# Delta-rule heads: token-major outputs, squares summed by ScalarE, modulation tiles turned for VectorE, and the filling shifted

## The chip, the cores and the metric

One core of a Trainium2 chip runs the kernel. The metric is the device time of one execution in microseconds, as a median of several. The core's engines run side by side, each through its own queue in order: TensorE (PE) for products and transposes, VectorE (DVE), ScalarE (ACT), GpSimd (POOL), and SyncE (SP), which issues most of the transfers. They meet by semaphores.

## The reference

Two transformer blocks over 512 tokens of width 1024. The change lies in the first block's mixer, a gated delta rule with 8 heads of width 128:

```python
qkv = jax.nn.silu(causal_depthwise_conv(p[..., Q_OFF:Z_OFF], gdn_conv_w))
q = l2_normalize(qkv[..., Q_OFF:K_OFF].reshape(b, s, GDN_HEADS, GDN_DK))
k = l2_normalize(...)
v = ...
g = -jnp.exp(a_log) * jax.nn.softplus(p[..., A_OFF:BETA_OFF] + dt_bias)
beta = jax.nn.sigmoid(p[..., BETA_OFF:SCB_OFF])
o = gated_delta_rule_chunked(q, k, v, g, beta)
o = rms_norm(o, gdn_norm_w) * jax.nn.silu(z)
```

In each chunk a triangular system is inverted (t_inv), and then a state of 128 x 128 is carried from chunk to chunk; o is the output. Six rows of modulation per block come from mod = c_act @ w_ada + b_ada, and a final pair from w_ada_f.

## The kernel before, in words

The heads run one after the other: a loop over heads 0 to 6 (stage HEAD), then head 7 written out (stage LAST). Within a head the 512 tokens are four chunks of 128 columns; part(v, n) is chunk n of a [128, 512] tile, bank(b) is one of eight PSUM banks of 512 floats. q, k and v lie with their channels on the partitions (gd q_s, k_s, v_s).

TensorE goes through PE_STEPS in order: kv_tokens (k and v transposed to token rows), g_rows, kk_qk, kb_rows, x_pairs (gd_u_t transposed), then for six levels n the steps y_n, x_n, u_n that invert the triangular matrices by doubling, w, then for each chunk v_new and o, then o_sums (the sum over channels of the squared output, four products with one moving column, and in the same bank six more with one column that sum ada_s, the modulation products that GpSimd has multiplied and added up), and o_norm_rows (the norm factors S_ON spread over rows by four transposes). Every step counts up the semaphore g_pe; the other engines have lists of their own (DVE_STEPS, ACT_STEPS, POOL_STEPS) with g_dve, g_act and g_pool.

Between these steps TensorE does filling: products that the next head (or the gates) needs, with a list of how many quarters stand ahead of which step (HEAD_FILL, LAST_FILL). A weight tile is [128, 8, 128] in two parts w_hi and w_lo and gives 24 products of 512 columns, in four quarters of six. The loop's head has eight tiles, 32 quarters. Tile t writes bank t % 2. The first quarter of a tile waits for the tile's w_lo and for the bank: out_used[b] counts how often the bank's content was consumed.

```python
if q == 0:
    pe.wait_ge(lo_ready, tile.before + 1)
    open_out(stage.out(j, i))
```

Tiles 1, 2 and 3 of a loop head are q, k and v of the next head. Their consumers are a scaled copy by ScalarE (conv_tap) and three taps by VectorE (conv_taps), each of which adds a shifted multiple of the bank to the copy; the third counts up out_used. On VectorE the q taps stand behind the copy of y1 (n == 1), the k taps behind the copy of x2, the v taps behind the copy of y4. Tiles 4 and 5 are the short convolution's, tile 6 a gate (tanh by ScalarE), tile 7 is z. Counted from 0, the quarters 5 to 7 stand at x_pairs, 8 at y0, 9 at x0, 10 at y1, 11 at x1, 12 at y2, 13 at x2 and so on; 12 opens tile 3.

The steps of the output: ScalarE squares o (channel-major, bank 3) into gd dec, VectorE adds the square of q, TensorE sums over channels, VectorE adds a constant (o_mean), GpSimd raises to -1/2 (o_norm), TensorE spreads it over rows into bank 6, and VectorE multiplies o by z and then by bank 6 (o_gate, o_scale), splits the product into og_hi and og_lo. In between it splits w_lo of a coming tile (ahead).

Of the kernel before, what the change touches and what calls it, by code (L numbers as in the profile page):

```python
# [187 lines left out]
LAST_FILL = dict(HEAD_FILL, y1=2, y2=2, y3=2, y4=2, y5=2, v_new0=2, o_sums=3)  # L190
# [44 lines left out]
def block_kernel(nc, a, out):  # L235
# [41 lines left out]


# [5 lines left out]
    with ctx:  # L284
# [396 lines left out]


# [39 lines left out]
        def _(act):  # L722
# [165 lines left out]
            def head(stage, i, h):  # L888
# [1643 lines left out]
```

## Time and profile before

| | us |
|---|---|
| median of 3 runs | 2262.08 |
| lowest, highest | 2258.78, 2263.14 |
| span of the profiled execution | 2261.5 |
| TensorE busy | 2186.9 (97%) |
| VectorE busy | 1319.8 (58%) |
| ScalarE busy | 851.1 (38%) |
| GpSimd busy | 550.0 (24%) |

The heads lie from about 96 us to 708 us of the span. The page's shares are means over stages; a timeline gives each instruction's start and duration and, in brackets, how long its engine had been idle ahead of it and what released it. Matmuls overlap, so their pace is read from start to start: two filling products are 0.23 us apart though each is shown as 0.39 us long. PEclk in a window is the granted TensorE clock as a share of 2.4 GHz.

### The profile page before, as it was taken

To read this page: it belongs to the slowest core of one execution; us is meant where nothing else is said; L and a number is where in the kernel's file an instruction comes from. 1 tells how busy PE (TensorE), PEld (TensorE's weight loads), DVE (VectorE), ACT (ScalarE), POOL (GpSimd) and SP (SyncE) were. 2 spreads that over 40 slices of the span, in tenths; PEclk is the share of its full clock that TensorE was granted. 3 is DMA by queue.
4 is the path that set the end of the run, shared out by engine and by line. 5 is a ranking of instruction groups with operands and counts; after the bars stand their busy time and mean duration, and the time that the engine had idled before them with its cause. 6 is when DMAs were issued, how large, how long until landed. Compare 5 with 4: busy or idle time off the path is not lost.

```text
span 2261.5 us, 30878 instructions
## 1 busy us (share of the span) xinstructions
PE 2186.9 (97%) x10744; PEld 1803.5 (80%) x10744; DVE 1319.8 (58%) x1846; ACT 851.1 (38%) x1248; POOL 550.0 (24%) x571
## 2 busy tenths in 40 slices
PE   5799999999999999999999999999899999999998
PEld 3688888888888878888888888888777777888886
DVE  6667666766654444434457665544588867656432
ACT  3232323233223223223224554532466645445322
POOL 0378777777770040000010000001000000000011
PEclk8899999999999999999999999999999999999999
DMA  6333333333333332333332333333211123333332
GB/s 245 119 102 101 93 97 111 89 96 98 112 94 93 112 112 84 93 102 93 93 94 86 101 95 95 98 96 93 65 57 57 54 68 93 94 102 93 95 96 70
DMA packets 352577, 216.97 MB, mean 96 GB/s; under 512 B 8648, under 2 KB 342914, under 8 KB 350979
## 3 DMA queue, kind: packets, MB, share of 16 engines
q1 hardware_dynamic: 344019, 188.47, 28.3%
q0 software_dynamic: 7968, 27.27, 4.1%
q8 instruction: 39, 0.64, 0.1%
q10 hardware_dynamic: 528, 0.40, 0.1%
q14 instruction: 23, 0.19, 0.0%
HBM read 211.92 MB, written 4.19 MB: 96 GB/s over the span
## 4 chain that ended last, share of the span: by engine, by line
PE 80%; DVE 12%; issue 3%; ACT 2%; DMA 1%; SPq 0%; DVEq 0%; POOL 0%; POOLq 0%; ACTq 0%
PE ps L2027 23%; PE ps L2029 23%; PE ps L2028 23%; PE ps L2198 5%; DVE w_lo L1202 2%; PE ps L2054 1%; DVE small L1911 1%; DMA ada<-w_ada 1%; DVE a_sb L1944 1%; DVE a_t_lo L1920 1%; ACT at_swap L1105 1%; DVE gd_q_g L1498 1%; DVE prob L1939 1%; DVE gd_q_s L1398 1%; DVE gd_y_t L1510 1%
## 5 line engine op out<-in xcount | busy, mean ns | idle before, releaser
L2027 PE MATMUL ps<-h_hi,w_hi 128*128 128x512 f32 x1896 | 773.5, 408 | 15.9 <-DVE gd_q_s L1398 6.3
L2029 PE MATMUL ps<-h_hi,w_lo 128*128 128x512 f32 x1896 | 746.9, 394 | 0.0
L2028 PE MATMUL ps<-h_lo,w_hi 128*128 128x512 f32 x1896 | 745.3, 393 | 0.0
L1202 DVE TENSOR_TENSOR w_lo<-raw,w_hi 128x1024 fp32r<-128x1024 f32 x336 | 452.6, 1348 | 364.3 <-ACT w_hi L730 363.7
L730 ACT ACTIVATE w_hi<-raw 128x1024 fp32r<-128x1024 f32 x336 | 355.5, 1059 | 637.4 <-PE ps L2029 602.3
L2027 PEld LDWEIGHTS ps<-h_hi,w_hi 128*128 128x128 f32 x1896 | 361.2, 190 | 90.2 <-issue 21.9
L2029 PEld LDWEIGHTS ps<-h_hi,w_lo 128*128 128x128 f32 x1896 | 359.7, 190 | 78.0
L2028 PEld LDWEIGHTS ps<-h_lo,w_hi 128*128 128x128 f32 x1896 | 361.3, 191 | 65.6
L2027 PE MATMUL ps<-act_hi,w_hi 128*128 128x512 f32 x528 | 206.0, 390 | 0.0
L2029 PE MATMUL ps<-act_hi,w_lo 128*128 128x512 f32 x528 | 205.5, 389 | 0.0
L2028 PE MATMUL ps<-act_lo,w_hi 128*128 128x512 f32 x528 | 205.4, 389 | 0.0
L598 POOL TENSOR_TENSOR sq_sum<-x 128x512 f32<-128x512 f32 x4 | 4.2, 1039 | 758.6 <-DVE x L1738 488.6
L639 POOL TENSOR_TENSOR ada_w<-ada_w 128x256 f32<-128x256 f32 x144 | 131.9, 916 | 11.3
L2029 PEld LDWEIGHTS ps<-act_hi,w_lo 128*128 128x128 f32 x528 | 99.1, 188 | 20.8
L2027 PEld LDWEIGHTS ps<-act_hi,w_hi 128*128 128x128 f32 x528 | 99.1, 188 | 20.5
L2028 PEld LDWEIGHTS ps<-act_lo,w_hi 128*128 128x128 f32 x528 | 99.1, 188 | 20.1
L639 POOL TENSOR_TENSOR ada_w<-ada_w,cact 128x512 f32<-128x512 f32 x96 | 110.3, 1149 | 3.1 <-DMA ada_w<-w_ada 2.0
L930 ACT ACTIVATE gd_u_t<-ps 128x512 f32<-128x512 f32 x48 | 28.7, 598 | 181.8 <-PE ps L2198 181.8
L1694 DVE TENSOR_TENSOR tmp<-ps,sq_tmp 128x512 f32<-128x512 f32 x44 | 30.4, 691 | 89.3 <-PE ps L2029 82.7
L602 POOL TENSOR_TENSOR sq_tmp<-x 128x512 f32<-128x512 f32 x24 | 25.9, 1079 | 232.6 <-DVE x L1738 149.2
L632 POOL DMA_DIRECT2D ada_w<-w_ada x64 | 51.0, 797 | 83.2 <-DVE g_tok L1381 41.7
L712 POOL TENSOR_TENSOR small<-small 128x4 f32<-128x4 f32 x8 | 8.1, 1007 | 252.4 <-DVE small L1970 252.4
(352 smaller groups left out, 2839.7 us busy)
## 6 DMA issues: line engine op xcount, KB each, us to landing
raw<-ffn_w_up SPq DMA_DIRECT2D x88, 512.0 KB, 3.8
raw<-w_in SPq DMA_DIRECT2D x72, 512.0 KB, 3.8
raw<-w_ffn_in SPq DMA_DIRECT2D x44, 512.0 KB, 3.8
ada_w<-w_ada POOLq DMA_DIRECT2D x64, 256.0 KB, 3.4
raw<-ffn_w_down SPq DMA_DIRECT2D x32, 512.0 KB, 3.7
raw<-diff_w_qkv SPq DMA_DIRECT2D x24, 512.0 KB, 3.7
ada<-w_ada SPq DMA_DIRECT2D x8, 1024.0 KB, 13.3
ada_w<-w_ada_f POOLq DMA_DIRECT2D x32, 256.0 KB, 3.3
```

What stands on the lines that cost most here:

```text
L602: nc.gpsimd.tensor_tensor(sq_tmp[:], x[:, m], x[:, m], MULT).then_inc(sq_own, 1)
L632: nc.gpsimd.dma_start(ada_w[:, half], src).then_inc(ada_land[half], 16)
L639: nc.gpsimd.tensor_tensor(dst, a, b, op).then_inc(ada_own, 1)
L730: nc.scalar.activation(w_hi[:, tile.slot], raw[:, tile.raw], ACT.Copy).then_inc(hi_ready, 1)
L930: nc.scalar.activation(gd["u_t"][:], bank(6), ACT.Copy).then_inc(g_act, 1)
L1105: swapped = nc.scalar.activation(at["swap"][32 * q:32 * q + 32], ps[32 * (q ^ 1):32 * (q ^ 1) + 32, b, :], ACT.Copy)
L1202: nc.vector.tensor_tensor(w_lo[:, tile.slot], raw[:, tile.raw], w_hi[:, tile.slot].bitcast(F32), SUB)\
L1694: nc.vector.tensor_tensor(gs, bank(b), sq_tmp[:], MULT).then_inc(out_used[b], 1)
L2027: nc.tensor.matmul(dst, w_hi[:, tile.slot, k], hi, start=first, stop=False)
L2028: nc.tensor.matmul(dst, w_hi[:, tile.slot, k], lo, start=False, stop=False)
L2029: return nc.tensor.matmul(dst, w_lo[:, tile.slot, k], hi, start=False, stop=last)
L2198: ins = nc.tensor.matmul(part(bank(b), n), part(lhs, n), part(rhs, n), start=True, stop=True)
```

## The change

Each output chunk is now token-major (tokens on the partitions), in a bank of its own (O_BANK). Its squares are summed by ScalarE along the row (accum_out), and so are those of q, for which q is transposed to token rows as well (q_tokens, bank 7, behind x_pairs). So o_norm needs no product; the factor S_ON is one number per partition and chunk, VectorE applies it (o_scale), TensorE transposes the result back (o_turn), and VectorE multiplies by z (o_gate). ada_s is transposed by TensorE (ada_turns) and summed along the row by VectorE. GpSimd waits for ada_turns ahead of the next head. Of the filling, one quarter goes from the end of the head to x_pairs: x_pairs has 4, and ada_turns, in the place of o_sums, has 1.

```diff
-PE_STEPS = ["kv_tokens", "g_rows", "kk_qk", "kb_rows", "x_pairs"]
+PE_STEPS = ["kv_tokens", "g_rows", "kk_qk", "kb_rows", "x_pairs", "q_tokens"]
...
-ACT_STEPS = ["k_squares", "exp_decay", "exp_g", "exp_g_rows", "exp_last", "exp_left", "q_squares", "x_pairs"]
+ACT_STEPS = ["k_squares", "exp_decay", "exp_g", "exp_g_rows", "exp_last", "exp_left", "x_pairs", "q_squares"]
...
-    DVE_STEPS += [f"y{_n}"] + (["kbeg_scale", "v_beta", "k_beg"] if _n == 0 else []) + _x
+    DVE_STEPS += [f"y{_n}"] + (["kbeg_scale", "v_beta", "k_beg"] if _n == 0 else ["q_sum"] if _n == 1 else []) + _x
...
-PE_STEPS += ["o_sums", "o_norm_rows"]
-DVE_STEPS += ["o_sum", "o_mean", "ada", "ada_f", "o_gate", "g_col", "o_scale", "o_lo"]
-
-
-
-HEAD_FILL = {name: 1 for name in PE_STEPS if name not in [f"u{_n}" for _n in range(LEVELS - 1)]}
-HEAD_FILL.update(kb_rows=2, x_pairs=3, o_sums=2)
-LAST_FILL = dict(HEAD_FILL, y1=2, y2=2, y3=2, y4=2, y5=2, v_new0=2, o_sums=3)
+PE_STEPS += ["ada_turns", "o_turn"]
+DVE_STEPS += ["o_mean", "ada_sum", "ada_f_sum", "ada", "ada_f", "o_scale", "g_col", "o_gate", "o_lo"]
+
+
+
+HEAD_FILL = {name: 1 for name in PE_STEPS if name not in ["q_tokens"] + [f"u{_n}" for _n in range(LEVELS - 1)]}
+HEAD_FILL.update(kb_rows=2, x_pairs=4)
+LAST_FILL = dict(HEAD_FILL, y1=2, y2=2, y3=2, y4=2, y5=2, v_new0=2, ada_turns=2)
 LAST_FILL["w"] = LAST_FILL["u5"] = 1
-LAST_FILL["o_norm_rows"] = 40 - (sum(LAST_FILL.values()) - LAST_FILL["o_norm_rows"])
+LAST_FILL["o_turn"] = 40 - (sum(LAST_FILL.values()) - LAST_FILL["o_turn"])
...
+    O_BANK = (3, 5, 6, 7)
...
+                pool.wait_ge(g_pe, step(PE_STEPS, "ada_turns", h))
...
-                nc.scalar.activation(gd["q_sq"][:], gd["q_s"][:], ACT.Square, scale=P * 1e-3).then_inc(g_act, 1)
...
+                after_pe("q_tokens")
+                for n in range(NC):
+                    q_sq = nc.scalar.activation(part(gd["q_sq"], n), part(bank(7), n), ACT.Square, scale=(P * EPS) ** 0.5,
+                                                accum_out=small[:, S_QSQ + n:S_QSQ + n + 1])
+                q_sq.then_inc(g_act, 1)
...
-                after_pe(f"o{NC - 1}")
-                nc.scalar.activation(gd["dec"][:], bank(3), ACT.Square).then_inc(g_act, 1)
+                for n in range(NC):
+                    after_pe(f"o{n}")
+                    o_sq = nc.scalar.activation(part(gd["dec"], n), part(bank(O_BANK[n]), 0), ACT.Square,
+                                                accum_out=small[:, S_OSQ + n:S_OSQ + n + 1])
+                o_sq.then_inc(g_act, 1)
...
-                after_dve("o_scale")
+                after_dve("o_gate")
...
+                    if n == 1:
+                        after_act("q_squares")
+                        nc.vector.tensor_scalar(col4(S_QSQ), col4(S_QSQ), P * EPS * 4 * EPS, None, ADD).then_inc(g_dve, 1)
...
-                nc.vector.tensor_tensor(gd["dec"][:], gd["dec"][:], gd["q_sq"][:], ADD).then_inc(g_dve, 1)
-                after_pe("o_sums")
-                nc.vector.tensor_scalar(col4(S_OMS), bank(5)[:, 0:NC], P * EPS * 4 * EPS, None, ADD).then_inc(g_dve, 1)
-                nc.vector.tensor_tensor(mod[:, bass.ds(4 * h + 16, 4)], bank(5)[:, 8:12],
+                nc.vector.scalar_tensor_tensor(col4(S_OMS), col4(S_OSQ), 1.0 / P, col4(S_QSQ), MULT, ADD).then_inc(g_dve, 1)
+                after_pe("ada_turns")
+                nc.vector.tensor_reduce(small[:, S_ADA:S_ADA + 4], chunks(bank(2)), AX_X, ADD).then_inc(g_dve, 1)
+                nc.vector.tensor_reduce(small[:, S_ADA + 4:S_ADA + 6], chunks(bank(4))[:, 0:2], AX_X, ADD).then_inc(g_dve, 1)
+                own("ada_sum")
+                nc.vector.tensor_tensor(mod[:, bass.ds(4 * h + 16, 4)], small[:, S_ADA:S_ADA + 4],
                                         vec[:, bass.ds(4 * h + (V_BADA + 16), 4)], ADD).then_inc(g_dve, 1)
-                nc.vector.tensor_tensor(mod[:, bass.ds(2 * h + 48, 2)], bank(5)[:, 12:14],
+                own("ada_f_sum")
+                nc.vector.tensor_tensor(mod[:, bass.ds(2 * h + 48, 2)], small[:, S_ADA + 4:S_ADA + 6],
                                         vec[:, bass.ds(2 * h + V_BADAF, 2)], ADD).then_inc(g_dve, 1)
-                dve.wait_ge(cv_dve, 10 * h + 10)
-                nc.vector.tensor_tensor(gd["low"][:], bank(3), gd["z_g"][:], MULT).then_inc(g_dve, 1)
+                dve.wait_ge(g_pool, step(POOL_STEPS, "o_norm", h))
+                nc.vector.tensor_scalar(part(gd["low"], 0), part(bank(O_BANK[0]), 0), small[:, S_ON:S_ON + 1], None, MULT)
+                nc.vector.tensor_tensor(chunks(gd["low"][:])[:, 1:NC], ps[:, O_BANK[1]:O_BANK[1] + NC - 1, 0:P],
+                                        spread(col4(S_ON))[:, 1:NC], MULT).then_inc(g_dve, 1)
                 nc.vector.tensor_copy(col4(S_G), head_cols(g_tok, h + 1 if more else h)).then_inc(g_dve, 1)
                 if more:
                     ahead(6)
-                after_pe("o_norm_rows")
-                own("o_gate")
-                nc.vector.tensor_tensor(gd["low_d"][:], gd["low"][:], bank(6), MULT).then_inc(g_dve, 1)
+                dve.wait_ge(cv_dve, 10 * h + 10)
+                after_pe("o_turn")
+                nc.vector.tensor_tensor(gd["low_d"][:], bank(6), gd["z_g"][:], MULT).then_inc(g_dve, 1)
...
-                pe.wait_ge(g_dve, last_head("o_gate", h))
+                pe.wait_ge(g_dve, last_head("o_scale", h))
...
-                pe.wait_ge(g_dve, last_head("o_scale", h))
+                pe.wait_ge(g_dve, last_head("o_gate", h))
...
+                by_chunk(7, q_s, None, True).then_inc(g_pe, 1)
...
-                        nc.tensor.matmul(part(bank(3), n), state[:], part(gd["q_g"], n), start=True, stop=False)
-                    o = nc.tensor.matmul(part(bank(3), n), part(y_t, n), part(gd["qk_t"], n), start=n == 0, stop=True)
+                        nc.tensor.matmul(part(bank(O_BANK[n]), 0), part(gd["q_g"], n), state[:], start=True, stop=False)
+                    o = nc.tensor.matmul(part(bank(O_BANK[n]), 0), part(gd["qk_t"], n), part(y_t, n), start=n == 0, stop=True)
...
-                fill("o_sums")
-                after_dve("o_sum")
-                for n in range(NC):
-                    nc.tensor.matmul(bank(5)[:, n:n + 1], part(gd["dec"], n), cst[:, C_MEAN:C_MEAN + 1], start=True, stop=True)
+                fill("ada_turns")
                 pe.wait_ge(g_pool, step(POOL_STEPS, "ada", h))
                 for j in range(6):
-                    s = nc.tensor.matmul(bank(5)[:, 8 + j:9 + j], ada_s[:, j], one_col, start=True, stop=True)
-                s.then_inc(g_pe, 1)
-                fill("o_norm_rows")
-                pe.wait_ge(g_pool, step(POOL_STEPS, "o_norm", h))
-                rows_of(6, S_ON).then_inc(g_pe, 1)
+                    t = turn(part(bank(2 if j < 4 else 4), j % 4), ada_s[:, j])
+                t.then_inc(g_pe, 1)
+                fill("o_turn")
+                after_dve("o_scale")
+                by_chunk(6, gd["low"], None, True).then_inc(g_pe, 1)
```

TensorE, loop head, the places around step x1. gd_x_t,gd_dia is the end of the products y1, gd_y_t,gd_u_t and gd_u_t,gd_y_t are x1 and u1. Before, from the last filling product at x1 on:

```order
L2028 MATMUL ps<-h_lo,w_hi 128x512
L2029 MATMUL ps<-h_hi,w_lo 128x512
L2188 REGISTER_ALU
L2191 REGISTER_ALU [waits g_dve]
L2198 MATMUL ps<-gd_y_t,gd_u_t 128x128 [waits g_act]
L2198 MATMUL ps<-gd_y_t,gd_u_t 128x128 x3
L2198 MATMUL ps<-gd_u_t,gd_y_t 128x128 x4
L2036 REGISTER_ALU
L2027 MATMUL ps<-h_hi,w_hi 128x512 [waits out_used1,lo_ready]
L2028 MATMUL ps<-h_lo,w_hi 128x512
L2029 MATMUL ps<-h_hi,w_lo 128x512
```

Now, from the products y1 on:

```order
L2207 REGISTER_ALU [waits g_pool]
L2217 MATMUL ps<-gd_x_t,gd_dia 128x128 [waits g_dve]
L2217 MATMUL ps<-gd_x_t,gd_dia 128x128 x3
L2055 REGISTER_ALU
L2046 MATMUL ps<-h_hi,w_hi 128x512 [waits out_used1,lo_ready]
L2047 MATMUL ps<-h_lo,w_hi 128x512
L2048 MATMUL ps<-h_hi,w_lo 128x512
L2046 MATMUL ps<-h_hi,w_hi 128x512
L2047 MATMUL ps<-h_lo,w_hi 128x512
L2048 MATMUL ps<-h_hi,w_lo 128x512
L2207 REGISTER_ALU
```

The filling product that waits for out_used1, the first of tile 3, stood behind x1 and u1 and now stands ahead of them, right behind y1.

VectorE, the same place: gd_y_t<-ps,cst copies the result of y1, and the L1398 rows are the three q taps. Before:

```order
L1510 TENSOR_TENSOR gd_y_t<-ps,cst 128x512 [waits g_pe]
L1393 ISA
L1398 ISA [waits cv_act]
L1398 SCALAR_TENSOR_TENSOR gd_q_s<-ps,vec,gd_q_s 128x511
L1397 ISA
L1398 ISA [waits cv_dve]
L1398 SCALAR_TENSOR_TENSOR gd_q_s<-ps,vec,gd_q_s 128x510
L1397 REGISTER_ALU
L1398 ISA [waits cv_dve]
L1398 SCALAR_TENSOR_TENSOR gd_q_s<-ps,vec,gd_q_s 128x509
```

Now (the taps are L1408):

```order
L1520 TENSOR_TENSOR gd_y_t<-ps,cst 128x512 [waits g_pe]
L1471 REGISTER_ALU
L1523 TENSOR_SCALAR small<-small 128x4 [waits g_act]
L1403 ISA
L1408 ISA [waits cv_act]
L1408 SCALAR_TENSOR_TENSOR gd_q_s<-ps,vec,gd_q_s 128x511
L1407 ISA
L1408 ISA [waits cv_dve]
L1408 SCALAR_TENSOR_TENSOR gd_q_s<-ps,vec,gd_q_s 128x510
L1407 REGISTER_ALU
L1408 ISA [waits cv_dve]
L1408 SCALAR_TENSOR_TENSOR gd_q_s<-ps,vec,gd_q_s 128x509
```

The taps stay where they were, with one small addition (q_sum) ahead of them.

TensorE, end of a loop head. Before, the end of the filling at o_sums and the two sums:

```order
L2028 MATMUL ps<-h_lo,w_hi 128x512
L2029 MATMUL ps<-h_hi,w_lo 128x512
L2188 REGISTER_ALU
L2266 MATMUL ps<-cst,gd_dec 128x1 [waits g_dve]
L2266 MATMUL ps<-cst,gd_dec 128x1 x3
L2267 REGISTER_ALU
L2269 MATMUL ps<-cst,ada_s 128x1 [waits g_pool]
L2269 MATMUL ps<-cst,ada_s 128x1 x5
```

Now, behind the one quarter at ada_turns, its transposes, the quarter at o_turn and the transposes of gd_low:

```order
L2284 REGISTER_ALU
L2073 MATMUL ps<-cst,ada_s 128x128 [waits g_pool]
L2073 MATMUL ps<-cst,ada_s 128x128 x5
L2046 MATMUL ps<-h_hi,w_hi 128x512
L2047 MATMUL ps<-h_lo,w_hi 128x512
L2048 MATMUL ps<-h_hi,w_lo 128x512
L2046 MATMUL ps<-h_hi,w_hi 128x512
L2047 MATMUL ps<-h_lo,w_hi 128x512
L2048 MATMUL ps<-h_hi,w_lo 128x512
L2207 REGISTER_ALU
L2073 MATMUL ps<-cst,gd_low 128x128 [waits g_dve]
L2073 MATMUL ps<-cst,gd_low 128x128 x3
```

The ten products of one column are gone, and the last transposes wait for g_dve (o_scale) in place of g_pool (o_norm).

## Rows read from the trace of the kernel before

**Rows 1.** The page, busy time by engine and the chain that ended last, by engine.

```profile
PE 2186.9 (97%) x10744; PEld 1803.5 (80%) x10744; DVE 1319.8 (58%) x1846; ACT 851.1 (38%) x1248; POOL 550.0 (24%) x571
...
PE 80%; DVE 12%; issue 3%; ACT 2%; DMA 1%; SPq 0%; DVEq 0%; POOL 0%; POOLq 0%; ACTq 0%
```

**Rows 2.** Windows: stretch, us, busy us and instructions by engine, clock, DMA.

```profile
319.60:394.40 74.80, 73.78 (x432) 63.10 (x431) 51.00 (x79) 22.12 (x43) 57.00 (x63) 0.98 0.35 100
394.40:467.90 73.50, 72.55 (x433) 61.93 (x432) 50.24 (x76) 22.09 (x42) 56.26 (x62) 1.00 0.33 93
616.30:708.00 91.70, 91.02 (x505) 77.90 (x504) 45.39 (x74) 28.09 (x39) 49.00 (x55) 0.98 0.30 86
386.50:390.00 3.50, 3.50 (x12) 2.75 (x11) 2.36 (x5) 1.19 (x2) 3.34 (x4) 0.52 0.24 54
```

**Rows 3.** Timeline of TensorE, end of a head: start, us, instructions [idle, releaser].

```profile
457.93 0.95 PE L2266 MATMUL ps<-cst,gd_dec 128*128 128x1 f32 x8
...
460.08 0.49 PE L2027 MATMUL ps<-h_hi,w_hi 128*128 128x512 f32 x1
```

**Rows 4.** Timeline of TensorE around the gd_u_t transposes and the step y1.

```profile
403.09 0.39 PE L2029 MATMUL ps<-h_hi,w_lo 128*128 128x512 f32 x1
403.81 0.65 PE L2054 MATMUL ps<-cst,gd_u_t 128*128 128x128 f32 x4 [0.34 <-DVE gd_u_t L1495]
404.22 0.48 PE L2027 MATMUL ps<-h_hi,w_hi 128*128 128x512 f32 x1
...
411.47 1.05 PE L2198 MATMUL ps<-gd_x_t,gd_dia 128*128 128x128 f32 x8
412.28 0.48 PE L2027 MATMUL ps<-h_hi,w_hi 128*128 128x512 f32 x1
...
415.85 0.47 PE L2027 MATMUL ps<-h_hi,w_hi 128*128 128x512 f32 x1 [0.15 <-DVE gd_q_s L1398]
```

**Rows 5.** Groups by line and shape, TensorE, seven loop heads: busy, mean ns | idle before.

```profile
L2198 PE MATMUL ps<-gd_y_t,gd_u_t 128*128 128x128 f32 x280 | 38.3, 280 | 2.3 <-DVE gd_y_t L1510 1.8
```

**Rows 6.** Timeline of VectorE around the step y1.

```profile
412.56 0.69 DVE L1510 TENSOR_TENSOR gd_y_t<-ps,cst 128x512 f32<-128x512 f32 x1 [1.45 <-PE ps L2198]
413.17 0.74 DVE L1398 SCALAR_TENSOR_TENSOR gd_q_s<-ps,vec,gd_q_s 128x511 f32<-128x511 f32 x1
414.06 1.64 DVE L1398 SCALAR_TENSOR_TENSOR gd_q_s<-ps,vec,gd_q_s 128x510 f32<-128x510 f32 x2 [0.15 <-DVE gd_q_s L1398]
...
416.21 3.02 DVE L1202 TENSOR_TENSOR w_lo<-raw,w_hi 128x1024 fp32r<-128x1024 f32 x1
```

**Rows 7.** The tap line L1398, who waited for it: us, times.

```profile
  PE ps L2027: 6.3, 8
```

**Rows 8.** Timeline of TensorE behind three waits outside the heads.

```profile
74.29 0.77 PE L2027 MATMUL ps<-h_hi,w_hi 128*128 128x512 f32 x1 [5.19 <-DVE gd_q_s L1398]
...
79.12 0.56 PE L2029 MATMUL ps<-h_hi,w_lo 128*128 128x512 f32 x1
...
90.44 0.50 PE L2027 MATMUL ps<-h_hi,w_hi 128*128 128x512 f32 x1 [2.58 <-ACT gd_th L869]
...
846.34 0.76 PE L2027 MATMUL ps<-h_hi,w_hi 128*128 128x512 f32 x1 [2.53 <-DVE h_lo L1266]
...
850.74 0.47 PE L2028 MATMUL ps<-h_lo,w_hi 128*128 128x512 f32 x1
```

**Rows 9.** Timeline of ScalarE and of GpSimd at the end of a head.

```profile
455.37 0.60 ACT L966 ACTIVATE gd_dec<-ps 128x512 f32<-128x512 f32 x1 [9.37 <-PE ps L2258]
...
457.47 0.79 POOL L632 DMA_DIRECT2D ada_w<-w_ada  x1 [1.45 <-issue]
460.51 1.03 POOL L680 TENSOR_TENSOR small<-small 128x4 f32<-128x4 f32 x1 [2.25 <-DVE small L1581]
```

**Rows 10.** Timeline of ScalarE in the last head, behind the step u4.

```profile
659.43 0.60 ACT L930 ACTIVATE gd_u_t<-ps 128x512 f32<-128x512 f32 x1 [6.19 <-PE ps L2198]
...
660.87 0.59 ACT L886 ACTIVATE x<-ps 128x512 f32<-128x512 f32 x1
```

More of the change, by code:

```diff
@@ L75 @@
 S_POOL, S_SHSQ, S_SQX = 68, 72, 73
+S_OSQ, S_QSQ, S_ADA = 80, 84, 88
 S_MAX, S_NEG, S_SUM, S_REC, S_L = 16, 20, 24, 28, 32
@@ L182 @@
     DVE_STEPS += [f"v_new{_n}"] + ([f"state{_n}"] if _n < NC - 1 else [])
-PE_STEPS += ["o_sums", "o_norm_rows"]
-DVE_STEPS += ["o_sum", "o_mean", "ada", "ada_f", "o_gate", "g_col", "o_scale", "o_lo"]
-HEAD_FILL = {name: 1 for name in PE_STEPS if name not in [f"u{_n}" for _n in range(LEVELS - 1)]}
-HEAD_FILL.update(kb_rows=2, x_pairs=3, o_sums=2)
-LAST_FILL = dict(HEAD_FILL, y1=2, y2=2, y3=2, y4=2, y5=2, v_new0=2, o_sums=3)
+PE_STEPS += ["ada_turns", "o_turn"]
[3 more added lines that the diff above has]
+LAST_FILL = dict(HEAD_FILL, y1=2, y2=2, y3=2, y4=2, y5=2, v_new0=2, ada_turns=2)
 LAST_FILL["w"] = LAST_FILL["u5"] = 1
-LAST_FILL["o_norm_rows"] = 40 - (sum(LAST_FILL.values()) - LAST_FILL["o_norm_rows"])
+LAST_FILL["o_turn"] = 40 - (sum(LAST_FILL.values()) - LAST_FILL["o_turn"])
 LAST_FILL["tail"] = 8
-assert sum(HEAD_FILL.values()) == 32 and sum(LAST_FILL.values()) == 48 and LAST_FILL["o_norm_rows"] in (1, 2)
+assert sum(HEAD_FILL.values()) == 32 and sum(LAST_FILL.values()) == 48 and LAST_FILL["o_turn"] in (1, 2)
 ATT_PE = ["scores0", "scores1", "v_turn", "scores2", "scores3"] + [f"turn{_q}" for _q in range(NC)] + ["pv", "sums", "rows"]
@@ L309, in block_kernel @@
         cact = sb("cact", [P, 2, KD])
-        small = sb("small", [P, 80])
+        small = sb("small", [P, 96])
         alog = sb("alog", [P, H])
@@ L932, in head @@
                     if more and n == 0:
-                        after_pe("kk_qk")
                         after_dve("q_g")
@@ L978, in head @@
                     ahead(7)
-                    after_dve("o_gate")
                     act.wait_ge(sc_dve, 3 * h + 3)
```

## The prediction

> **What bounds the kernel now.** I read the page's busy shares and its chain first [rows 1]: TensorE is busy 97% of the span, and the chain that ended last runs through it for 80%. So a change counts by what it does to TensorE's own sequence: work put on it or taken off, and stretches in which it waits. The other engines matter through the waits alone. Next the windows of single head iterations [rows 2]: one takes 73.50 us at a granted clock of 1.00, or 74.80 us at 0.98. The difference of 1.3 us has a place. Right behind the products with one moving column (the o sums and the ada sums) the clock reads 0.52 for a stretch, which is the 1.2 GHz level beside the usual 2.4. Four of the seven loop iterations read 74.8 or 74.9 us and 0.98 in this way (one of them stands in the rows), and the last head, too, reads 0.98: five such stretches in all. Last I read TensorE's timeline through one iteration for the waits that are left in it [rows 4, 5].
>
> **Own work of TensorE, per head.** Removed: the o sums and the ada sums, from 457.93 to the next filling product at 460.08 [rows 3], 2.15 us. Added: six transposes of ada_s and four of q_s. Four transposes take 0.41 us start to start (403.81 to 404.22) [rows 4], so ten take 1.03. The four transposes of S_ON and the four of gd_low cost the same and cancel; the o products swap their operands and keep count and shape. Sum: -1.1 us a head, -8.8 us for eight, all of it on the path. (The Trainium skill, TensorE: Matmul & The Clock Gate, section Terms, calls the transpose mode four times faster for FP32. The row shows 0.10 us for a transpose, and eight FP32 passes of 128 columns, four products, take 0.81 (411.47 to 412.28) [rows 4], so here it is twice. With the page's factor the ten would cost 0.5 us and the kernel would end 4 us earlier. I go by the row.)
>
> **The filling that moves.** This is the term that decides. A head's filling is 32 quarters of six products, four quarters to a weight tile; tiles go to banks 0 and 1 in turn. The first quarter of a tile waits until the bank's last tile has been consumed. With x_pairs at 4 in place of 3, each later quarter stands one slot earlier, and so does each of those waits. I went through them tile by tile. Tile 3 (bank 1) opened at y2, behind the products x1 and u1. Now it opens at x1, right behind y1. Bank 1 is released by the third q tap of VectorE, which stands on VectorE behind the copy of y1 to gd_y_t. The rows give the price: the y1 products start at 411.47 and TensorE is free again at 412.28, 0.81 later [rows 4]. VectorE copies y1 from 412.56 and runs the three taps from 413.17 to about 415.7 [rows 6]; TensorE's next filling starts at 415.85 [rows 4] and names the tap as what it waited for, as it does in all seven heads and once before them [rows 7]. So the bank comes free 4.38 us after y1's start, which the shift of the filling doesn't change, since VectorE waits for y1 itself. New wait: 4.38 - 0.81 = 3.57, and the small q_sum that now stands between copy and taps adds some 0.07: **+3.6 us a head**, seven times. Before, x1, u1 and a quarter of filling lay over it and 0.15 was left idle (0.3 start to start).
>
> Tile 4 (bank 0) opens at x3 in place of y4, and waits for the k taps in the same way, but from x2 there lie u2, a quarter and y3 on TensorE (0.89 + 0.81 + 1.4 + 0.9 = 4.0 us) against 1.1 + 0.6 + 2.65 = 4.35 us on VectorE: +0.3. Tiles 5 to 7 are consumed several microseconds before their new slots. In the last head tile 3 waits for the first step of the short convolution (about 0.3) and tile 6 for the tanh on ScalarE behind u4, which ends 660.87 + 0.59 while u4's copy starts at 659.43 [rows 10], against one quarter and y5's first on TensorE: about +0.9 once.
>
> Waits that go: the transposes of gd_u_t start 0.72 us after the filling product ahead of them, not 0.23 (403.09 to 403.81) [rows 4]: 0.49, which the fourth quarter covers. The waits for gd_y_t at x0 and x2 are 2.3 us in seven heads as idle [rows 5]; idle reads 0.15 less than start to start at each, so 0.55 a head. With the 0.3 at tile 3: -1.3 us a head.
>
> **The end of a head.** Before, no wait stood ahead of the rows of S_ON in most heads. Now TensorE does a quarter, six transposes, a quarter, and then needs gd_low. Counted from the end of the last o product: the last square, a quarter of the 0.60 us square of before with an accumulator read behind it [rows 9], 0.4 as an estimate, o_mean 0.2, the power on GpSimd 1.03 [rows 9], so S_ON is there at about 1.8. But o_scale stands on VectorE behind the ada sums, which wait for the transposes: 1.46 + 0.65 + 0.25 to see them = 2.35; two reductions of 512 and 256 elements from PSUM at the pace of the y copy (0.61 for 512 [rows 6]) 0.95; two small adds, each behind a wait, 0.35; o_scale in two pieces 0.7; 0.1 to TensorE: 4.45. TensorE is there at 1.46 + 0.65 + 1.46 = 3.6. New wait **+0.85 a head** (0.3 to 1.4). In the last head o_turn has two quarters and covers it. The squares, now in pieces with accumulator reads, lie on ScalarE, idle there for 9.37 us before; the added 0.5 us is hidden.
>
> **The clock.** The products of one column go, and with them the five half-speed stretches at 1.3 us: -6.5. The new wait of 3.6 us takes their place. Rows on idling: after 5.19 us of waiting for the same tap ahead of the heads, the products run slowly from 74.29 to 79.12, eleven gaps of 0.44 us where 0.23 is usual; after 2.53 us of idling they do so from 846.34 to 850.74 [rows 8]. That is half speed for 4.4 to 4.8 us, 2.2 us lost; behind the thin products 1.3 us was lost. I take 1.7 for each of seven heads: +11.9. (The Trainium skill, TensorE: Matmul & The Clock Gate, section HAM oscillation — how this bites in real kernels, says that idle gaps drop the clock again and that each costs a slow restart; the two gaps of rows 8 agree. By that rule all seven waits pay.)
>
> **Sum.** A loop head: -1.1 - 1.3 + 3.6 + 0.3 + 0.85 = +2.35; seven: +16.4. Clock: 11.9 - 5.2 = +6.7. Last head: -1.1 - 0.8 (old waits) - 1.3 + 0.3 + 0.9 = -2.0. Total +21. The profiled execution is its span of 2261.5 us, 0.6 under the median of 2262.08, so 2261.5 + 21 = 2282.5; I say **2282**.
>
> **Rivals.**
> - No half speed after the waits: one wait of 2.58 us, ahead of 90.44, was followed by products at the usual pace [rows 8], so the clock does not answer every gap. Then 2261.5 + 16.4 - 5.2 - 2.0 = 2271. At 2.2 us for each it is 2286.
> - The new wait isn't there, because bank 1 comes free before y1. Then the kernel gets faster: -8.8 own work, -1.0 a head of old waits (-8), -6.5 of clock, +0.85 x 7 = +6: 2261.5 - 17 = 2244. GpSimd takes a little of it back: its last ada transfer is issued at 457.47 and lasts 0.79 [rows 9], till 458.26, while the transposes would be due near 458.1. For it: TensorE's idle at that place is 0.15 us only. Against it: VectorE's order puts the taps behind the copy of y1, and that copy waits for y1. It decides if the wait stays under 0.4 us a head.
> - The wait is there but half as long, as VectorE catches up, and the clock holds: 16.4 - 7 x 1.8 - 5.2 - 2.0 = -3.4, 2258 to 2262, no change to be seen.
> - VectorE gets later, not earlier: its copies into SBUF share time with GpSimd's sums (w_lo took 3.02 us at 416.21 [rows 6]); if o_scale and the taps are each 0.5 us later, +7: 2290.
>
> **Chances.** Forecast with the clock at 1.3 to 2.2 us a wait 0.72; full speed after the waits 0.10; later VectorE 0.06; half wait 0.05; no wait 0.07. A measurement of this kernel tells about 0.2% (4.5 us) from no change. Faster 0.07, same 0.05, slower 0.88. The range runs from full speed after the waits, with 3 us for the terms' error, to the late VectorE: 2268 to 2292.
>
> **What would show it.** In each loop head of the changed profile an idle of about 3.4 us ahead of the filling behind y1, released by the q tap; a granted clock near 0.5 behind it, and none behind the ada transposes; no wait at the gd_u_t transposes; about 0.7 us idle ahead of the gd_low transposes, released by VectorE; loop heads of about 76.5 to 77.5 us against 73.5 to 74.8. I am wrong if the bank's release comes from somewhere ahead of y1, if the clock falls for longer than the stretches seen, or if o_scale is more than 1.4 us late.

## The result, and the profile after

The changed kernel takes 2272.67 us (median of four, 2271.41 to 2279.05) against 2262.36: a ratio of 1.0048, 95% interval 1.0035 to 1.0061. It is slower, as forecast and inside the range, but by 10.3 us where the forecast had 20. Its profiled execution has a span of 2269.3 us, 7.8 more than the one before.

The page after, with the parts that answer to [rows 1]:

```profile
PE 2170.7 (96%) x10664; PEld 1793.9 (79%) x10664; DVE 1319.2 (58%) x1870; ACT 861.4 (38%) x1360; POOL 538.1 (24%) x571
...
PE 86%; DVE 7%; issue 2%; ACT 2%; DMA 1%; SPq 1%; DVEq 0%; POOL 0%; POOLq 0%; ACTq 0%
```

TensorE is at 96% where it was at 97%, with less busy time (2170.7 us against 2186.9) in a longer span. So its work has shrunk and its waits have grown. The list of who waited for the tap line, now L1408, says for which (before: [rows 7]):

```profile
  PE ps L2046: 29.5, 8
```

29.5 us instead of 6.3. Of that 5.19 is the wait ahead of the heads, as before; the other seven are one for each loop head, about 3.5 us. TensorE's timeline through one head, in the columns of [rows 3, 4] (start, duration, instructions, idle and releaser):

```profile
410.13 0.60 PE L2073 MATMUL ps<-cst,gd_u_t 128*128 128x128 f32 x4
410.57 0.60 PE L2073 MATMUL ps<-cst,gd_q_s 128*128 128x128 f32 x4
...
417.83 1.05 PE L2217 MATMUL ps<-gd_x_t,gd_dia 128*128 128x128 f32 x8
422.36 0.47 PE L2046 MATMUL ps<-h_hi,w_hi 128*128 128x512 f32 x1 [3.47 <-DVE gd_q_s L1408]
...
465.49 0.82 PE L2073 MATMUL ps<-cst,ada_s 128*128 128x128 f32 x6
466.06 0.47 PE L2046 MATMUL ps<-h_hi,w_hi 128*128 128x512 f32 x1
...
468.69 0.66 PE L2073 MATMUL ps<-cst,gd_low 128*128 128x128 f32 x4 [1.00 <-DVE gd_low L1606]
```

Read from start to start: y1's products start at 417.83 and TensorE could go on 0.81 later, as before [rows 4]; the next filling starts at 422.36, that is 4.53 us after y1's start and 3.72 us later than it could. The gd_u_t transposes come without a wait. Six ada transposes take 0.57 us (465.49 to 466.06). The gd_low transposes start 1.00 us (idle) late. VectorE in the same two places:

```profile
418.92 0.69 DVE L1520 TENSOR_TENSOR gd_y_t<-ps,cst 128x512 f32<-128x512 f32 x1 [1.43 <-PE ps L2217]
419.53 0.24 DVE L1523 TENSOR_SCALAR small<-small 128x4 f32<-128x4 f32 x1
419.68 0.74 DVE L1408 SCALAR_TENSOR_TENSOR gd_q_s<-ps,vec,gd_q_s 128x511 f32<-128x511 f32 x1
420.57 1.64 DVE L1408 SCALAR_TENSOR_TENSOR gd_q_s<-ps,vec,gd_q_s 128x510 f32<-128x510 f32 x2 [0.15 <-DVE gd_q_s L1408]
...
466.34 0.69 DVE L1595 TENSOR_REDUCE small<-ps 128x4 f32<-128x512 f32 x1 [1.48 <-PE ps L2073]
466.95 0.41 DVE L1596 TENSOR_REDUCE small<-ps 128x2 f32<-128x256 f32 x1
467.28 0.56 DVE L1598 TENSOR_TENSOR mod<-small,vec 128x4 f32 x1
467.76 0.15 DVE L1601 TENSOR_TENSOR mod<-small,vec 128x2 f32 x1
467.83 0.34 DVE L1605 TENSOR_SCALAR gd_low<-ps,small 128x128 f32<-128x128 f32 x1
468.09 0.54 DVE L1606 TENSOR_TENSOR gd_low<-ps,small 128x384 f32<-128x384 f32 x1
```

The three taps follow the copy of y1 and the small q_sum; at the head's end o_scale (L1605 and L1606) comes last, behind the two reductions and two additions.

The loop as a whole went from 520.0 us (first k transposes at 92.0, the last head's at 612.0) to 528.8 (91.9 to 620.7): +8.8. The last head, up to the gates' first product, went from 94.0 to 92.0 us: -2.0. The rest, +1.0, lies behind the heads and was not traced; it varies by nearly as much between profiles of kernels that are the same there (+0.2 in experiment 1).

Last, the clock. Three head windows and two short ones behind the wait, in the columns of [rows 2]:

```profile
345.69:422.36 76.67, 72.14 (x421) 62.42 (x421) 50.61 (x81) 23.45 (x56) 55.40 (x63) 0.98 0.34 96
422.36:497.51 75.15, 70.61 (x421) 61.17 (x421) 50.62 (x81) 23.46 (x56) 55.42 (x63) 1.00 0.35 98
497.51:572.68 75.17, 70.65 (x420) 61.18 (x421) 50.63 (x81) 23.46 (x56) 55.39 (x63) 1.00 0.35 98
...
269.07:273.57 4.50, 4.50 (x21) 4.22 (x22) 1.07 (x2) 0.00 (x0) 3.08 (x5) 0.66 0.09 36
345.69:350.19 4.50, 4.50 (x20) 3.94 (x21) 0.41 (x1) 0.00 (x0) 3.08 (x5) 0.63 0.09 36
```

Of the seven waits, two are followed by a stretch in which the windows read 0.66 and 0.63: the engine fell to the 1.2 GHz level for part of them. Behind the other five the clock reads 1.00. A fall, here and below, is such a stretch at the 1.2 GHz level. Behind the ada step the clock no longer falls in any head.

### The profile page after: what moved, and what is told of

Same layout as the page of the kernel before. It is cut to its first block, busy times and chain, and to the rows that moved or that the text cites. A ratio compares the mean times of both kernels' runs of the same rounds, so it can differ in the third digit from the quotient of the medians.

```text
span 2269.3 us, 30869 instructions
## 1 busy us (share of the span) xinstructions
PE 2170.7 (96%) x10664; PEld 1793.9 (79%) x10664; DVE 1319.2 (58%) x1870; ACT 861.4 (38%) x1360; POOL 538.1 (24%) x571
## 4 chain that ended last, share of the span: by engine, by line
PE 86%; DVE 7%; issue 2%; ACT 2%; DMA 1%; SPq 1%; DVEq 0%; POOL 0%; POOLq 0%; ACTq 0%
PE ps L2046 25%; PE ps L2048 24%; PE ps L2047 24%; PE ps L2217 6%; PE ps L2073 2%; DMA ada<-w_ada 1%; DVE w_lo L1212 1%; DVE gd_q_s L1408 1%; DVE a_t_lo L1939 1%; DVE gd_k_s L1408 1%; ACT at_swap L1115 1%; DVE a_sb L1963 0%; PE ps L2505 0%; DVE small L1930 0%; PE ps L2459 0%
## 5 line engine op out<-in xcount | busy, mean ns | idle before, releaser
L2046 PE MATMUL ps<-h_hi,w_hi 128*128 128x512 f32 x1896 | 771.4, 407 | 40.6 <-DVE gd_q_s L1408 29.5
L1212 DVE TENSOR_TENSOR w_lo<-raw,w_hi 128x1024 fp32r<-128x1024 f32 x336 | 438.7, 1306 | 366.0 <-ACT w_hi L735 365.5
L642 POOL TENSOR_TENSOR ada_w<-ada_w 128x256 f32<-128x256 f32 x144 | 120.6, 838 | 11.3
```

Source lines behind the costliest of these rows:

```text
L642: nc.gpsimd.tensor_tensor(dst, a, b, op).then_inc(ada_own, 1)
L1212: nc.vector.tensor_tensor(w_lo[:, tile.slot], raw[:, tile.raw], w_hi[:, tile.slot].bitcast(F32), SUB)\
L2046: nc.tensor.matmul(dst, w_hi[:, tile.slot, k], hi, start=first, stop=False)
```

## The experiments

All times below stand against the kernel before as it ran beside them (2264.4 to 2264.5 us in the three batches), except where the changed kernel is named; its own 2272.67 ran beside 2262.36.

### 1. The filling put back

```diff
-HEAD_FILL.update(kb_rows=2, x_pairs=4)
-LAST_FILL = dict(HEAD_FILL, y1=2, y2=2, y3=2, y4=2, y5=2, v_new0=2, ada_turns=2)
+HEAD_FILL.update(kb_rows=2, x_pairs=3, ada_turns=2)
+LAST_FILL = dict(HEAD_FILL, y1=2, y2=2, y3=2, y4=2, y5=2, v_new0=2, ada_turns=3)
```

> The changed kernel with its filling put back: x_pairs has 3 quarters again and ada_turns 2, so tile 3 opens at y2. Theory A, the bank: the loop heads of the changed kernel (75.16 us at full clock, the wait behind y1 3.63 start to start) lose that wait and the 0.21 at x3 and get back the small waits of before (0.49 + 0.23 + 0.32 + 0.38 + 0.22 + 0.28 = 1.92): 73.2 us a head, no half-speed stretch, 2271.5 - 7 x 1.92 - 3 = about 2255 us. Theory B, the new end of the head and the work moved to VectorE and ScalarE are what costs: the filling hardly matters, 2266 to 2273 us.

Measured: 2252.9 us (2252.38 to 2253.31), ratio 0.9949 (0.9932 to 0.9965). TensorE's timeline at the same step:

```profile
407.20 1.05 PE L2217 MATMUL ps<-gd_x_t,gd_dia 128*128 128x128 f32 x8
...
410.36 1.06 PE L2217 MATMUL ps<-gd_u_t,gd_y_t 128*128 128x128 f32 x8
411.65 0.47 PE L2046 MATMUL ps<-h_hi,w_hi 128*128 128x512 f32 x1 [0.24 <-DVE gd_q_s L1408]
```

and the window of this head, in the columns of [rows 2]:

```profile
385.80:458.80 73.00, 71.13 (x421) 60.85 (x420) 51.79 (x81) 23.41 (x57) 57.02 (x62) 1.00 0.36 101
```

Tile 3 opens 0.24 us late, not 3.47; a head takes 73.00 us at full clock. The rest of the change, without the shift, is a gain of 11.6 us, so the shift costs some 22 us in the changed kernel. Theory A stands, theory B falls. The wait ahead of gd_low (1.01) is still there.

### 2. The shift alone

```diff
-HEAD_FILL.update(kb_rows=2, x_pairs=3, o_sums=2)
-LAST_FILL = dict(HEAD_FILL, y1=2, y2=2, y3=2, y4=2, y5=2, v_new0=2, o_sums=3)
+HEAD_FILL.update(kb_rows=2, x_pairs=4, o_sums=1)
+LAST_FILL = dict(HEAD_FILL, y1=2, y2=2, y3=2, y4=2, y5=2, v_new0=2, o_sums=2)
```

> The kernel before with the filling's shift alone: x_pairs 4, o_sums 1. Theory A: each loop head gets a wait of 3.6 us behind y1 and 0.2 at x3 and loses 1.9 us of small waits, +1.9 x 7 = +13; the half-speed stretches behind the one-column products stay (4 x 1.3) and one to three more come behind the wait: 2274 to 2281 us. Theory B: 2260 to 2264 us, as before.

Measured: 2290.8 us, ratio 1.0118 (1.0101 to 1.0135), 26 us slower and 10 above the top of what was expected. TensorE's timeline at the step, and below it windows of a head, behind the wait and behind the one-column products:

```profile
351.22 1.05 PE L2198 MATMUL ps<-gd_x_t,gd_dia 128*128 128x128 f32 x8
355.60 0.47 PE L2027 MATMUL ps<-h_hi,w_hi 128*128 128x512 f32 x1 [3.33 <-DVE gd_q_s L1398]
```

The windows, whose eighth figure is the granted clock:

```profile
329.40:407.70 78.30, 74.77 (x432) 64.84 (x431) 50.20 (x79) 22.36 (x43) 55.31 (x62) 0.96 0.33 94
433.85:438.35 4.50, 4.50 (x19) 4.04 (x20) 0.45 (x1) 0.00 (x0) 3.70 (x5) 0.62 0.19 58
403.81:406.78 2.97, 2.97 (x10) 2.35 (x9) 2.17 (x4) 0.15 (x1) 2.89 (x3) 0.50 0.06 9
```

The wait is what was expected. But half speed follows it in seven heads of seven, though it is no longer than in the changed kernel (3.33 against 3.47 us idle), and it follows the one-column products in six of the seven loop heads, where the kernel before has it in four. A loop head takes 78.3 us: 73.5, +1.9 for the waits and two falls at about 1.45; the last one, which has only the fall behind the wait, takes 76.8. The wait's size was right and the count of falls wrong.

### 3. The q taps ahead of the copy of y1

```diff
+                    if more and n == 1:
+                        conv_taps(stage, 1, i, 0, h + 1)
                     after_pe(f"y{n}")
...
-                    if more and n == 1:
-                        conv_taps(stage, 1, i, 0, h + 1)
```

> The changed kernel with the three q taps ahead of VectorE's copy of y1 instead of behind it; nothing else. Theory A: they can start when ScalarE's scaled copy is there, bank 1 comes free about 1.8 us earlier, the wait falls from 3.6 to about 1.8 us in each of seven heads, and with idle that short no half-speed stretch follows: 2271.5 - 12.6 - 3 = about 2256 us. If half speed follows an idle of 1.8 us as often as one of 3.5 us, 2259 us and two stretches in the profile. Theory B: no change, 2271 us.

Measured: 2270.32 us (ten runs), ratio 1.0028 (1.0018 to 1.0037), some 4 us under the changed kernel where each is set against its own kernel before. TensorE's timeline:

```profile
419.62 0.47 PE L2046 MATMUL ps<-h_hi,w_hi 128*128 128x512 f32 x1 [1.79 <-DVE gd_q_s L1408]
...
432.02 0.50 PE L2046 MATMUL ps<-h_hi,w_hi 128*128 128x512 f32 x1 [1.27 <-DVE gd_k_s L1408]
```

and VectorE's around them, with two of GpSimd's rows:

```profile
419.38 0.68 DVE L1522 TENSOR_TENSOR gd_y_t<-ps,cst 128x512 f32<-128x512 f32 x1
419.98 2.48 DVE L1525 TENSOR_SCALAR small<-small 128x4 f32<-128x4 f32 x1
420.13 1.31 POOL L674 TENSOR_TENSOR gd_dia<-gd_low,masks 128x512 f32<-128x512 f32 x1
421.38 1.05 POOL L642 TENSOR_TENSOR ada_w<-ada_w,cact 128x512 f32<-128x512 f32 x1
422.38 0.68 DVE L1548 COPY gd_x_t<-ps 128x512 f32<-128x512 f32 x1
...
425.93 2.98 DVE L1416 SCALAR_TENSOR_TENSOR gd_q_s<-gd_th,gd_q_s 128x512 f32<-128x512 f32 x1
```

The wait is down to 1.79 us, and no fall of the clock follows it in any head. But the gain went into a new wait: TensorE stands 1.27 us for the k taps, and 0.7 us more later on. The VectorE rows show why: q_sum, 128 x 4 elements, took 2.48 us on the mean of seven heads, and the sum at L1416 2.99, where the changed kernel has 0.24 and 1.28 us for them. Both read and write SBUF alone; the copies from PSUM around them keep their 0.68. GpSimd works through its mask and modulation products at that time. (The Trainium skill, SBUF — State Buffer, section SBUF: two separate sides, says that a VectorE instruction in a two-port mode, or one with two SBUF inputs beside a GpSimd instruction that reads SBUF, and GpSimd exclude one another for a whole instruction. The rows agree in this: what reads PSUM isn't touched. The length they show is more: q_sum starts 0.15 us ahead of GpSimd's mask product and ends 0.03 us behind the modulation product after it, so it lasted over two GpSimd instructions. Whether q_sum is in a two-port mode no row shows.) The expectation had moved an engine's work and not asked what it would then stand beside.

### 4. A longer wait

```diff
                     if more and n == 1:
+                        for c in (77, 78, 79):
+                            nc.vector.tensor_reduce(small[:, c:c + 1], bank(4), AX_X, ADD)
                         conv_taps(stage, 1, i, 0, h + 1)
```

> The changed kernel with three reductions of 512 elements (results unused) on VectorE between the copy of y1 and the q taps, some 0.6 us each: the wait behind y1 grows from 3.6 to 5.4 us. Theory A: +1.8 x 7 = +13 us. For the clock: if a longer idle makes the fall certain, all seven heads pay about 2.2 us and the time is 2271.5 + 13 - 3 + 15 = about 2296 us; if the fall stays as rare as at 3.5 us of idle (two heads in seven), about 2284 us. Theory B (the wait is hidden by something else that is late): under 2275 us.

Measured: 2293.27 us, ratio 1.0129 (1.0112 to 1.0146). One of the seven waits in TensorE's timeline:

```profile
278.62 0.77 PE L2048 MATMUL ps<-h_hi,w_hi 128*128 128x512 f32 x1 [5.27 <-DVE gd_q_s L1408]
```

The window that starts with it:

```profile
278.62:283.12 4.50, 4.50 (x20) 3.92 (x21) 0.41 (x1) 0.00 (x0) 1.35 (x3) 0.63 0.21 58
```

All seven waits are followed by half speed. 1.8 us a head and five more falls than in the changed kernel give 20 us; measured, each against its own kernel before, 18.5. The wait is on the path in full.

### 5. The factor ahead of the sums, filling still shifted

The same lines in another order on VectorE, and the list of steps to match:

```diff
-DVE_STEPS += ["o_mean", "ada_sum", "ada_f_sum", "ada", "ada_f", "o_scale", "g_col", "o_gate", "o_lo"]
+DVE_STEPS += ["o_mean", "o_scale", "ada_sum", "ada_f_sum", "ada", "ada_f", "g_col", "o_gate", "o_lo"]
...
-                pe.wait_ge(g_dve, last_head("o_scale", h))
+                pe.wait_ge(g_dve, last_head("ada_f", h))
```

> The changed kernel with VectorE applying the norm factor (o_scale) ahead of the sums of the ada tiles instead of behind them; the filling stays shifted. The wait of 1.17 us ahead of the gd_low transposes goes in seven heads: -8 us, and a loop head at full clock takes 74.0 us. Theory C on the clock (the length of the idle behind y1, 3.5 us, alone sets how often half speed follows, two heads in seven): 2264 us. Theory D (where the wait falls in time decides as well, since the same wait was followed by half speed in seven heads of seven at 78.3 us a head and in two of seven at 75.2): another count than two, up to 2272 us with seven stretches, 2261 with none.

Measured: 2270.54 us (2268.38 to 2275.44, seven runs), ratio 1.0029 (1.0018 to 1.0041). The profiled run is the longest of them, 2275.44. TensorE's timeline at the wait behind y1 and at the gd_low transposes:

```profile
348.46 0.47 PE L2046 MATMUL ps<-h_hi,w_hi 128*128 128x512 f32 x1 [3.47 <-DVE gd_q_s L1408]
...
395.23 0.60 PE L2073 MATMUL ps<-cst,gd_low 128*128 128x128 f32 x4
```

The windows behind two of the waits:

```profile
348.46:352.96 4.50, 4.50 (x19) 4.04 (x20) 0.44 (x1) 0.00 (x0) 3.07 (x5) 0.62 0.10 39
574.40:578.90 4.50, 4.50 (x20) 3.92 (x21) 0.37 (x1) 0.00 (x0) 3.07 (x5) 0.62 0.09 36
```

The wait ahead of gd_low is gone, as meant. The wait behind y1 is unchanged, and in this run half speed followed in seven heads of seven (clock 0.50 in the first window and 0.62 in six). In the profiled run the saved 1.17 us a head was paid back as falls of the clock; by the medians some 4 of the 8 us came through. So the length of the idle alone doesn't decide: theory C falls. Another count than two is what theory D said, but that it is the place in time that changes it is argued, not shown.

### 6. Both

Experiments 1 and 5 in one kernel.

> The filling put back (x_pairs 3, ada_turns 2) and o_scale ahead of the ada sums. From 2252.9 us with the filling back, the wait of 1.17 us ahead of the gd_low transposes goes in each of seven heads: 2252.9 - 8.2 = 2244.7 us, loop heads of 71.8 us and no half-speed stretch. If GpSimd's modulation sums come later than TensorE then wants them, a wait ahead of the ada transposes takes 0.3 to 0.8 us of it back: 2247 to 2250 us.

Measured: 2243.86 us (2243.15 to 2244.51), ratio 0.9907 (0.9890 to 0.9924); 71.5 us a head and no fall. The two repairs add up here (9.0 us for the second), where in experiment 5 the second was worth little. GpSimd is not late.

### 7. The ada tiles by one-column products again

```diff
-                    t = turn(part(bank(2 if j < 4 else 4), j % 4), ada_s[:, j])
+                    t = nc.tensor.matmul(bank(2)[:, j:j + 1], ada_s[:, j], one_col, start=True, stop=True)
...
-                nc.vector.tensor_reduce(small[:, S_ADA:S_ADA + 4], chunks(bank(2)), AX_X, ADD).then_inc(g_dve, 1)
-                nc.vector.tensor_reduce(small[:, S_ADA + 4:S_ADA + 6], chunks(bank(4))[:, 0:2], AX_X, ADD).then_inc(g_dve, 1)
```

The two additions read the bank. The filling is put back as in experiment 1.

> The filling put back, and the ada tiles summed by six products of one moving column as before the change (no transposes, no reductions on VectorE); the rest of the change stays. TensorE's own work is +0.8 us a head, the wait ahead of gd_low falls from 1.17 to about 0.2: about -0.2 us a head. Theory E (a run of one-column products, here 1.3 us and not 2.2 with the o sums, is enough for a fall of the clock): half-speed stretches in about half the heads, 2252.9 + 4 = 2257 us. Theory F (it takes the longer run, or a wait): none, 2251 to 2253 us.

Measured: 2251.64 us (2251.46 to 2254.8), ratio 0.9947 (0.9930 to 0.9963), against 2252.9 in experiment 1.

```profile
379.10 1.39 PE L2282 MATMUL ps<-cst,ada_s 128*128 128x1 f32 x12
380.35 0.48 PE L2042 MATMUL ps<-h_hi,w_hi 128*128 128x512 f32 x1
...
381.81 0.65 PE L2069 MATMUL ps<-cst,gd_low 128*128 128x128 f32 x4
```

The six products take 1.25 us and the clock falls behind none of them. That is theory F: only the longer run (2.15 us with the o sums) was followed by falls; but this kernel's heads are shorter too, 72.5 us, and the two aren't separated. Turning the ada tiles gains nothing while o_scale stands behind their sums: it saves 0.7 us on TensorE and gives more than that back in the wait for VectorE (heads of 73.0 us against 72.5 here).

### 8. A quarter from kb_rows to x_pairs, tile 3 still at y2

```diff
-HEAD_FILL.update(kb_rows=2, x_pairs=3, ada_turns=2)
+HEAD_FILL.update(x_pairs=4, ada_turns=2)
```

on the kernel of experiment 6.

> As the kernel with both (filling back, o_scale early), and one quarter of filling moved from kb_rows to x_pairs, so that x_pairs has four again while tile 3 still opens at y2: the lower triangle is asked for 1.4 us earlier. The wait of 0.49 us at the gd_u_t transposes goes in eight heads and nothing else moves: 2244.7 - 3.9 = about 2241 us. If S_KB isn't ready that much earlier, TensorE waits for it at kb_rows instead and the time stays at 2245 us or more.

Measured: 2242.66 us (2240.95 to 2242.96), ratio 0.9901 (0.9884 to 0.9918). Five loop heads are at 70.1 to 70.4 us and two at 74.1 and 75.2. In the longer of the two, VectorE:

```profile
313.89 0.69 DVE L1502 TENSOR_TENSOR gd_u_t<-gd_low,cst 128x512 f32<-128x512 f32 x1
314.62 4.06 DVE L1505 TENSOR_TENSOR gd_u_t<-gd_u_t,cst 128x512 f32<-128x512 f32 x1
...
328.26 1.94 DVE L1523 TENSOR_SCALAR small<-small 128x4 f32<-128x4 f32 x1
```

One addition of 128 x 512 in SBUF took 4.06 us (1.67 in most heads, 0.69 for its like just ahead of it), and q_sum behind it 1.94. TensorE waited 1.37 us for the one and 2.00 for the taps behind the other. In the other long head the same two operations take 4.09 and 1.94 us. Windows behind the wait for the taps in these two heads:

```profile
332.79:337.29 4.50, 4.50 (x17) 3.95 (x18) 2.15 (x3) 2.13 (x3) 0.66 (x2) 0.62 0.52 149
478.34:482.84 4.50, 4.50 (x27) 4.00 (x28) 3.48 (x4) 2.13 (x3) 2.04 (x3) 1.00 0.54 151
```

So an idle of 2.00 us was followed by half speed in one of them and 2.01 us in the other was not. That fall is the 1.2 us between the two heads.

### 9. A slower head

```diff
+                for _ in range(3):
+                    rows_of(4, S_G)
                 rows_of(4, S_G).then_inc(g_pe, 1)
```

on the changed kernel: 12 more transposes of the same values at g_rows.

> The changed kernel with three more repeats of the four transposes at g_rows in each head (same values, nothing reads them apart): TensorE's work grows by 12 transposes, 1.3 us a head, 76.5 us a head at full clock, and the wait of 3.6 us behind y1 stays. The idle in front of x1 is as long as in the changed kernel, only its place in time moves. Theory C (its length alone decides): two half-speed stretches as there, 2272 + 10.4 = 2282 us. Theory D (where the wait falls in time decides as well): another count; with seven 2290 us, with none 2279 us.

Measured: 2289.35 us (2288.96 to 2289.65), ratio 1.0111 (1.0095 to 1.0126). Half speed follows the wait in six heads of seven, all but the fifth; windows behind the fourth and the fifth wait:

```profile
355.51:360.01 4.50, 4.50 (x20) 4.19 (x21) 0.93 (x2) 0.00 (x0) 3.08 (x5) 0.64 0.10 42
433.58:438.08 4.50, 4.50 (x28) 4.02 (x29) 1.82 (x2) 1.06 (x3) 3.08 (x5) 1.00 0.11 42
```

The idle is 3.47 to 3.49 us in every head, as in the changed kernel, and the count is six in place of two. The fifth head takes 76.4 us and most others 78.1. This is the expectation of theory D in its form, not in a number: nothing told that it would be six.

### 10 and 11. q_sum behind the copy of y3

On the kernels of experiments 6 and 8, one line of VectorE moved from n == 1 to n == 3.

> The kernel with the filling back and o_scale early, with q_sum (one small addition on VectorE, which took up to 2.5 us beside GpSimd's sums) moved from between the copy of y1 and the q taps to behind the copy of y3. The bank of tile 3 comes free 0.07 us earlier in most heads: 2243.9 - 1 = about 2243 us. If the small addition is held up at its new place as well, TensorE hardly waits for it there: no loss.

> The same with the quarter moved from kb_rows to x_pairs. In the profile of that kernel without the move of q_sum five loop heads took 70.1 to 70.4 us and two took 74.1 and 75.2, where VectorE's additions in SBUF were held up beside GpSimd (u0 4.06 us, q_sum 1.94 us). With q_sum out of the way the second of the two is gone in part: 2242.7 - 2 to 2242.7 - 4 = about 2240 us; if u0's hold-up alone decides, 2242 us as before.

Measured: 2244.86 us (2242.99 to 2246.23), ratio 0.9916 (0.9903 to 0.9930), no gain over experiment 6; and 2237.41 us (2234.01 to 2241.81), ratio 0.9888 (0.9873 to 0.9904), 5 us under experiment 8 and the best of the study, 27 us under the kernel before. The intervals of the two ratios overlap, though three of its four runs lie below all of experiment 8's, so the gain over experiment 8 is likely and not shown. Its runs spread over 8 us: in the profile five heads stand at 69.9 to 70.1 us and two, in which the same addition in SBUF takes 4.1 us, at 71.7 and 72.1.

## Why the forecast came out as it did

**Its sign and its cause were right.** The decisive step, that a quarter moved to x_pairs opens tile 3 behind y1 and so ahead of the taps that free its bank, is confirmed by the releaser in all seven heads, by experiment 1 (take the shift back: 22 us on the changed kernel, set each against its own kernel before) and by experiment 2 (the shift alone: +26 us). Its price was +3.6 us and came out at 3.7; the 0.1 is q_sum, forecast at 0.07 us and 0.15 us from its start to the taps'.

**Term by term, a loop head at full clock.** Forecast +2.35 us, measured +1.6 (75.13 against 73.52).

| term | forecast | measured, start to start |
|---|---|---|
| own work of TensorE | -1.1 | -1.2 |
| waits that go | -1.3 | -2.4 |
| tile 3 behind y1 | +3.6 | +3.7 |
| tile 4 at x3 | +0.3 | +0.3 |
| gd_low transposes | +0.85 | +1.17 |

These rows sum to +1.6. The waits were under-counted. At the four places of the forecast they came to 1.7 us (0.49 at the gd_u_t transposes, 0.33 at x0, 0.40 at tile 3, 0.48 at x2). Two more, 0.32 us at y5 and 0.38 at the o products of chunk 2, were not in the list and went as well; a TensorE that is later gives VectorE time everywhere, which fits and isn't tested alone. The wait for gd_low was within its bounds. The 0.56 us that one of the two additions takes (467.28, where 0.15 is usual) is again an operation in SBUF beside GpSimd's first product.

**The last head** was forecast at -2.0 and is -2.0.

**The clock is the term that failed.** It was put at +6.7 us: seven falls at 1.7, less the four of before in the loop at 1.3. Measured: two falls, each worth 1.45 us (76.65 against 75.2 us a head), so 2.9 less 5.4, -2.5 us. That is 9 of the 14 us by which the loop was too high; the rest is 7 x 0.74, most of it the waits. The size of one fall was about right. The count wasn't. The step was to read that two long waits were followed by half speed, to note one of 2.58 us that was not, and then to take all seven. One of the two was no evidence. In the kernel before the clock was at half already ahead of the wait of 2.53 us that ends at 846.34 [rows 8]:

```profile
840.70:846.30 5.60, 1.11 (x4) 0.72 (x4) 3.30 (x5) 1.33 (x2) 1.94 (x1) 0.50 0.32 94
```

TensorE was busy for 1.11 us of these 5.6. So the rows had one fall, after 5.19 us, and one wait near 2.6 us without one, and none between. The full-speed case had 0.10, and the profiled run is nearer to it (2271 us) than to the forecast: that the measured time lies in the range owes as much to the range's lower end, set by that case, as to the sum. It was not a matter of a rule either way: the same idle of 3.3 to 3.5 us was followed by a fall in two heads of seven (changed kernel), six (experiment 9), and seven (experiments 2 and 5). In one kernel, too, the runs differ: the changed kernel's four spans are 2269.3, 2269.4, 2271.8 and 2276.9 us with mean clocks of 0.987, 0.987, 0.986 and 0.984, where the kernel of experiment 1, without a long wait, stays within 1 us. At 5.27 us all seven fell, at 1.79 none. What decides in between is open; these runs show that the count changes when a head gets longer or shorter and the idle does not; they don't show by what.

**The rivals.** "No wait" falls with the releaser rows. "Half wait" falls too: the idle is 3.47 us, not half of it. Experiment 3, which made it half as long by moving the taps, got back 4 of the 12.6 us, since other waits took its place; it doesn't test the rival's own way. "A later VectorE" was not seen in the changed kernel at the taps.

## What to carry to other kernels

When filler work is moved, don't count it as a block: write down for each piece what it waits for (here the bank), and walk through every later piece, since all of them shift by one slot. A wait that an engine's order hides exactly (0.15 us idle over a chain of 4.4) is the place that breaks. And a wait of a few microseconds on TensorE should be priced as itself plus a chance of a clock fall, from none to all, not as one number.

## What the runs showed of the hardware

- Half speed after an idle of TensorE: none in seven after 1.79 us (experiment 3); one of two after 2.0 us (experiment 8); two, six, seven and seven of seven after 3.3 to 3.5 us (the changed kernel, experiments 9, 2 and 5); seven of seven after 5.27 us (experiment 4). The wait of 2.6 us ahead of the loop, the same in all thirteen profiles, is followed by a fall in two, those of experiments 2 and 5 (clock 0.50 in 90.39:94.89 and in 90.36:94.86). Each fall in a loop head cost 1.2 to 1.7 us. One-column products: falls in four of seven heads after 2.15 us of them, six of seven in experiment 2, none after 1.25 us.
- Because of that a saving can vanish: experiment 5 took 1.17 us out of a head and the profiled run got five more falls for it.
- An addition of 128 x 512 floats in SBUF takes 0.69 us on VectorE by itself and up to 4.1 beside GpSimd (experiments 8 and 11), one of 128 x 4 from 0.15 to 2.5 us, while copies from PSUM keep their 0.68 us throughout. What stands behind such an operation inherits the delay.
